# One layer of a hybrid backbone on one NeuronCore: k's heads moved to banks that q's copies leave free, and GpSimd's subtractions cut in four

## The reference

```python
shift_a, scale_a, gate_a, shift_f, scale_f, gate_f = modulation(silu(c) @ w_ada + b_ada)   # w_ada: 1024 x 6144
h = rmsnorm(x, g_pre_mix) * (1.0 + scale_a) + shift_a
z = h @ w_in                                    # u | q | k | v | o, 512 columns each, and 16 gate columns
y_pool = pool_mixer(u, w_pool, pool_scale)      # box means over 2, 4, 8, 16 positions
y_ml, C, n, m = mlstm_mixer(q, k, v, o, gate_pre, b_gate, C0, n0, m0)   # 4 heads, forward and backward
x = x + gate_a * rmsnorm(concat(y_pool, y_ml) @ w_out, g_post_mix)
h = rmsnorm(x, g_pre_ffn) * (1.0 + scale_f) + shift_f
x = x + gate_f * rmsnorm(moe(h), g_post_ffn)    # 64 experts, top 6 of 4 groups, and one shared expert
```

## Time and profile before

| what | value |
|---|---|
| median of three runs | 725.77 us (725.65 to 727.65) |
| the profiled execution | 726.23 us, of which the span of the engines' work is 724.1 us |
| PE busy | 685.0 us, 95% of the span |
| DVE busy | 384.5 us, 53% |
| ACT busy | 194.1 us, 27% |
| POOL busy | 89.1 us, 12% |
| HBM | 254.64 MB read, 357 GB/s over the span |
| granted clock of PE, mean | 0.994 |

### The profile page before, as it was taken

The page is one execution under the profiler, slowest core; times in us unless marked ns, Lnnn a source line. Parts: engine busy times, 40 slices in busy tenths (PEclk is TensorE's granted clock), DMA queues, the critical chain, the costliest instruction groups (busy, mean ns, idle before and its releaser), DMA issues.

```text
span 724.1 us, 11495 instructions
## 1 busy us (share of the span) xinstructions
PE 685.0 (95%) x4263; PEld 395.1 (55%) x4263; DVE 384.5 (53%) x979; ACT 194.1 (27%) x335; POOL 89.1 (12%) x53
## 2 busy tenths in 40 slices
PE   2799999989999999999999999999999999999993
PEld 2588888767865735545444545454445445444431
DVE  3458989694298354454444445454445436442115
ACT  3245344563371302112111111211111121130103
POOL 2453655313213000000000000000000000000000
PEclk9999999999999999999999999999999999999997
DMA  9999875815489479999999999999999999999994
GB/s 316 382 350 340 260 245 221 296 55 175 146 329 426 204 290 417 428 423 427 393 386 428 421 425 424 423 425 424 425 424 427 423 425 426 423 426 421 419 410 189
DMA packets 51013, 259.16 MB, mean 358 GB/s; under 512 B 6704, under 2 KB 9312, under 8 KB 32904
## 3 DMA queue, kind: packets, MB, share of 16 engines
q1 hardware_dynamic: 46816, 252.50, 86.6%
q0 software_dynamic: 1584, 4.90, 2.0%
q10 hardware_dynamic: 2552, 0.98, 0.5%
HBM read 254.64 MB, written 3.71 MB: 357 GB/s over the span
## 4 chain that ended last, share of the span: by engine, by line
PE 66%; DMA 14%; DVE 12%; SPq 3%; issue 2%; ACT 2%; POOL 0%; DVEq 0%; ACTq 0%
PE psum L2495 22%; PE psum L2503 10%; PE psum L2383 9%; PE psum L2467 8%; DMA w_gu<-in_w_expert_gu 7%; DVE psum L1329 4%; DMA w_gu<-in_w_in 3%; PE psum L2344 3%; DMA w_dn<-in_w_expert_down 2%; DMA w_gu<-in_w_ada 2%; PE psum L2395 2%; SPq L800 1%; PE psum L604 1%; PE psum L2454 1%; PE psum L2067 1%
## 5 line engine op out<-in xcount | busy, mean ns | idle before, releaser
L2495 PE MATMUL psum<-w_gu,hgT 128*32 128x512 f32 (+1 forms) x1280 | 191.4, 594 | 2.5 <-DMA w_gu<-in_w_expert_gu 2.5
L2495 PEld LDWEIGHTS psum<-w_gu,hgT 128*32 128x32 f32 (+1 forms) x1280 | 57.9, 119 | 127.7 <-issue 127.6
L1782 DVE TENSOR_TENSOR f_acc<-f_acc,psum 128x512 f32<-128x512 f32 x132 | 86.7, 684 | 43.3 <-PE psum L2467 43.3
L2503 PE MATMUL psum<-w_dn,actT 128*32 128x512 f32 (+1 forms) x640 | 98.7, 596 | 1.4 <-DMA w_dn<-in_w_expert_down 0.9
L1760 DVE SCALAR_TENSOR_TENSOR act<-sil,wsl,psum 128x256 f32<-128x256 f32 x27 | 18.4, 681 | 127.6 <-ACT sil L1127 118.3
L589 POOL TENSOR_TENSOR w_lo<-w_gu,w_hi 128x2048 fp32r<-128x2048 f32 x13 | 59.9, 4606 | 71.4 <-ACT w_hi L881 71.4
L2383 PE MATMUL psum<-onehot,h_lo 128*128 128x512 f32 (+1 forms) x168 | 66.6, 397 | 0.0
L2383 PE MATMUL psum<-onehot,h_hi 128*128 128x512 f32 (+1 forms) x168 | 65.4, 389 | 0.0
L2503 PEld LDWEIGHTS psum<-w_dn,actT 128*32 128x32 f32 (+1 forms) x640 | 27.0, 119 | 58.5 <-issue 57.7
L1766 DVE TENSOR_TENSOR y_lo<-psum,y_hi 128x1024 fp32r<-128x1024 f32 x26 | 31.8, 1224 | 50.8 <-ACT y_hi L1131 50.8
L1127 ACT ACTIVATE sil<-psum 128x256 f32<-128x256 f32 x27 | 10.4, 384 | 173.7 <-PE psum L2495 173.7
(11 more groups left out here) (335 smaller groups left out, 846.5 us busy)
## 6 DMA issues: line engine op xcount, KB each, us to landing
w_gu<-in_w_expert_gu SPq DMA_DIRECT2D x49, 2048.0 KB, 17.3
w_dn<-in_w_expert_down SPq DMA_DIRECT2D x61, 1024.0 KB, 15.1
w_gu<-in_w_expert_gu SPq DMA_DIRECT2D x27, 1024.0 KB, 15.9
w_gu<-in_w_ada SPq DMA_DIRECT2D x12, 2048.0 KB, 13.4
w_gu<-in_w_in SPq DMA_DIRECT2D x4, 2048.0 KB, 10.2
w_gu<-in_w_out SPq DMA_DIRECT2D x2, 2048.0 KB, 9.0
bc<-mod_rows POOLq DMA_DIRECT2D x6, 512.0 KB, 7.3
w_gu<-in_w_expert_gu SPq DMA_DIRECT2D x6, 512.0 KB, 20.4
```

The source lines that it names most:

```text
L1782: v.tensor_tensor(dst, dst, bank(5 + n), ALU.add).then_inc(f_added, 1)
L2495: ins = t.matmul(bank(target)[rows, :], column(c)[:, rows], w_gu[s][:, c, :], start=(c == 0), stop=(c == NC - 1), tile_position=(0, rows.s ...
L2503: ins = t.matmul(bank(target + n)[rows, :], actT[:, j, rows], w_dn[s][:, j, 512 * n:512 * (n + 1)], start=(j == 0), stop=(j == 1), tile_po ...
```

## The change

1. `z_bank`: k's heads go to banks 4, 3, 2, 5 (before 2, 3, 4, 5), and v's, o's and u's tiles to 4, 3, 2 (before 2, 3, 4). Only k's third head now shares a bank with a head of q.
2. `ada(4)` is moved from between q and k to between the halves of k. Its result goes to bank 1 (before bank 6), and it waits for the first copy of q (before for DVE's `abs_ready`). On DVE `ada_sums(5)` goes ahead of `ada_evac(4)`.
3. `low` subtracts in four pieces of 128 x 512 (before one of 128 x 2048). PE still waits for all four pieces of a half. The last half of w1 is divided as before.
4. ACT rounds k's second half (`high(3)`) after two of q's four copies (before after all four).
5. `g_nat` is one tile of 72 rows: rows 0 to 3, 32 to 35 and 64 to 67 hold the backward rows of the three quantities (six DVE copies), and the four rows after each of these the forward rows, which three transfers on ACT's queue bring (before nine DVE copies). A token tile is then transposed by one product (before three), and two DVE copies put its columns in order (before one).

```diff
@@ z_bank
-            return (1, 2, 0, 7)[i] if w == "q" else 2 + i
+            return {"q": (1, 2, 0, 7), "k": (4, 3, 2, 5)}.get(w, (4, 3, 2))[i]
@@ low
+        PIECES = 4
...
-            cs = slice(4 * half, 4 * half + 4)
             engine.wait_ge(w_hi_ready, k + 1)
-            engine.tensor_tensor(w_lo[s][:, cs, :], w_gu[s][:, cs, :], w_hi[half][:, :, :].bitcast(F32), ALU.subtract)\
-                .then_inc(w_lo_ready, 1)
+            for j in range(PIECES):
+                c = 4 * half + j
+                engine.tensor_tensor(w_lo[s][:, c, :], w_gu[s][:, c, :], w_hi[half][:, j, :].bitcast(F32), ALU.subtract)\
+                    .then_inc(w_lo_ready, 1)
@@ scalar
-            for n in range(4):
-                z_evac(n)
+            z_evac(0)
+            z_evac(1)
             high(3)
+            z_evac(2)
+            z_evac(3)
...
+            a.wait_ge(w_ready, 2)
+            for n, rows in enumerate((g_u, g_b, g_t)):
+                a.dma_start(g_nat[32 * n + H:32 * n + 2 * H, :], rows[0:H, :]).then_inc(nat_ready, 16)
@@ vector
-            ada_evac(4)
             ada_sums(5)
+            ada_evac(4)
...
-                v.tensor_copy(g_nat[0:32, n, :], rows[0:32, :]).then_inc(nat_ready, 1)
-                v.tensor_copy(g_nat[32:36, n, 0:T_CTX], rows[32:36, natural(1, 0)]).then_inc(nat_ready, 1)
-                v.tensor_copy(g_nat[32:36, n, T_CTX:T], rows[32:36, T - 1:T_CTX - 1:-1]).then_inc(nat_ready, 1)
+                here = slice(32 * n, 32 * n + H)
+                v.tensor_copy(g_nat[here, 0:T_CTX], rows[32:36, natural(1, 0)]).then_inc(nat_ready, 1)
+                v.tensor_copy(g_nat[here, T_CTX:T], rows[32:36, T - 1:T_CTX - 1:-1]).then_inc(nat_ready, 1)
@@ tensor, ada
-                if i == 4:
-                    t.wait_ge(abs_ready, 1)
-                if i > 4:
-                    t.wait_ge(z_act, 4)
+                if i >= 4:
+                    t.wait_ge(z_act, 1 if i == 4 else 4)
@@ tensor, z_chunk
-                    t.wait_ge(w_lo_ready, SPLIT.index((w, half)) + 1)
+                    t.wait_ge(w_lo_ready, PIECES * (SPLIT.index((w, half)) + 1))
...
                     if half == 0:
                         ins.then_inc(half_used, 1)
+                        if w == "k":
+                            ada(4)
@@ tensor, gates_T
-                for a_ in range(3):
...
+                t.matmul(bank(1, col, col + 24), g_nat[:, P * tile:P * tile + P],
+                         ident[0:72, 0:96].rearrange("p (a r) -> p a r", a=3)[:, :, 0:2 * H],
+                         start=True, stop=True).then_inc(gT_done, 1)
```

More of the change, by code:

```diff
@@ L328, in build_layer @@
         w_pool = at("w_pool", [P, len(WINDOWS), P], BC + 21248)
-        g_nat = at("g_nat", [36, 3, T], BC + 15104)
+        g_nat = at("g_nat", [72, T], BC + 17408)
         bc = at("bc", [P, 6, D], BC)
@@ L357, in ada_direct @@
         def ada_direct(i):
-            j = 3 if i == 4 else i % 4
-            return bank(6 + i % 2, P * j, P * j + P)
+            if i == 4:
+                return bank(1, 0, P)
+            return bank(6 + i % 2, P * (i % 4), P * (i % 4) + P)
         def ada_out(i):
@@ L953, in _ @@
             high(7)
-            a.wait_ge(gT_ready, 1)
+            a.wait_ge(gT_ready, 2)
             a.activation(emT[:, :, :], gT[:, 1, :, :], ACT.Exp, scale=-1.0).then_inc(em_ready, 1)
@@ L1236, in _ @@
             own.add(v.memset(gate_sum[:, :], 0.0))
+            own.add(v.memset(g_nat[:, :], 0.0))
             own.add(v.memset(v1[:, :, :, DH:DV], 1.0))
@@ L1315, in ada_sums @@
                         v.wait_ge(z_act, 4)
-                        v.wait_ge(mod_ready, 5)
+                        v.wait_ge(abs_ready, 1)
                     elif i == 9:
@@ L1356, in _ @@
             v.tensor_tensor(g_b[:, :], g_b[:, :], g_mx[:, :], ALU.add).then_inc(scans_ready, 1)
+            ada_sums(5)
             ada_evac(4)
-            ada_sums(5)
             v.wait_ge(scans_ready, 1)
@@ L1367, in _ @@
             v.wait_ge(gT_done, NT)
-            v.tensor_copy(gT[:, :, :, :].rearrange("p a i r -> p (a i r)"), bank(1, T, T + 72)).then_inc(gT_ready, 1)
+            rows_T = bank(1, T, T + 72).rearrange("p (i a r) -> p a i r", i=NT, a=3)
+            for d in range(2):
+                v.tensor_copy(gT[:, :, :, H * d:H * d + H], rows_T[:, :, :, H * (1 - d):H * (1 - d) + H]).then_inc(gT_ready, 1)
             ada_evac(5)
@@ L1958, in _ @@
             g.wait_ge(mxhi_ready, 3)
-            g.wait_ge(w_lo_ready, 8)
+            g.wait_ge(w_lo_ready, PIECES * 8)
             for n, (rows, dst, src) in enumerate(MAXIMA):
@@ L2021, in ada_total @@
                 if i >= 6:
-                    t.wait_ge(gT_ready, 1)
+                    t.wait_ge(gT_ready, 2)
                 for m in range(2):
@@ L2086, in q_low @@
             def q_low(heads, half):
-                t.wait_ge(w_lo_ready, half + 1)
+                t.wait_ge(w_lo_ready, PIECES * (half + 1))
                 for h in heads:
@@ L2169, in z_chunk @@
                         ins.then_inc(half_used, 1)
+                        if w == "k":
+                            ada(4)
             def gates_T(tile):
-                t.wait_ge(nat_ready, 9)
-                for a_ in range(3):
-                    col = T + 24 * a_ + 8 * tile
-                    ins = t.matmul(bank(1, col, col + 2 * H), g_nat[:, a_, P * tile:P * tile + P],
-                                   ident[0:36, 0:64].rearrange("p (d r) -> p d r", d=2)[:, :, 0:H],
-                                   start=True, stop=True)
-                ins.then_inc(gT_done, 1)
+                t.wait_ge(nat_ready, 6 + 16 * 3)
+                col = T + 24 * tile
+                t.matmul(bank(1, col, col + 24), g_nat[:, P * tile:P * tile + P],
+                         ident[0:72, 0:96].rearrange("p (a r) -> p a r", a=3)[:, :, 0:2 * H],
+                         start=True, stop=True).then_inc(gT_done, 1)
             def keys_T():
@@ L2291, in wo_step @@
                     ins.then_inc(wo_done, 1)
-            t.wait_ge(w_lo_ready, SPLIT.index(("w0", 0)) + 1)
+            t.wait_ge(w_lo_ready, PIECES * (SPLIT.index(("w0", 0)) + 1))
             t.wait_ge(tl_ready, len(PARTS) + 1)
@@ L2313, in _ @@
             mixed_T(2)
-            t.wait_ge(w_lo_ready, SPLIT.index(("w0", 1)) + 1)
+            t.wait_ge(w_lo_ready, PIECES * (SPLIT.index(("w0", 1)) + 1))
             for i in range(NT):
@@ L2318, in _ @@
                 wo_step(0, 1, i)
-            t.wait_ge(w_lo_ready, SPLIT.index(("w1", 0)) + 1)
+            t.wait_ge(w_lo_ready, PIECES * (SPLIT.index(("w1", 0)) + 1))
             wo_step(1, 0, 0)
             wo_step(1, 0, 1)
-            t.wait_ge(w_lo_ready, LAST_HALF + 1)
+            t.wait_ge(w_lo_ready, PIECES * LAST_HALF + 1)
             t.wait_ge(w_lo_last, 1)
```

2 lines of the change are left out of this document (removed).

## The result

| | before | after |
|---|---|---|
| median | 725.75 us (20 runs) | 728.59 us (727.37 to 731.78, 20 runs) |
| ratio, 95% interval | | 1.0038 [1.0027, 1.0049] |
| profiled execution, its span | 726.23, 724.1 us | 728.84, 726.9 us |
| PE busy | 685.0 us | 685.0 us |
| POOL busy | 89.1 us, 12% | 97.2 us, 13% |

The changed kernel is slower by 2.8 us: inside the predicted range, but by its median past the 0.3% that "no change" was to mean (the interval begins at 0.27%). All of it is there when PE comes to `ada_total(9)`: from that point to the end of the span before took 593.8 us and after 593.6.

A forecast was written before the change was run, and what follows sets the result against it. PE's and DVE's chains were taken to end together at `ada_total(9)`, 0.51 us apart. PE starting o 1.3 us later, less that wait, gave 0.8 us slower: about 726.6 us median, range 723.8 to 728.9.

The forecast's parts named there:

- The pieces' own time: On POOL, a piece of 512 columns takes 1.27 us, four take 5.1 us, 0.5 us more than one subtraction.
- The charge for DVE's two operations: Two small DVE operations let in between pieces hold POOL up 0.35 us each, 0.7 us in all.
- What the pieces bring: DVE's long waits shrink to the rest of one piece, 0 to 1.3 us; scans end some 5 us earlier.
- 1.7 of the 1.9 us of removed gaps: Ahead of k and v on PE: POOL's slower pieces eat 1.7 us, leaving v 0.2 us earlier.
- k's start: On PE, k starts when POOL is done, at 55.8 us instead of 57.92, 2.1 us earlier.
- a4's move and SP: a6's issue 9.5 us later, landing and constants 5.2 us later; o issued at 79.5 us, started 1.3 us later.
- Rival A: SP's hanging issue falls away, o comes in time, PE goes on 1.5 us earlier: 723.9 us, chance 0.18.
- rival B: Queue serves o and a7 side by side, o lands in 12.2 us: 3.8 us slower, 729.6 us, chance 0.17.
- edits at nothing: g_nat's memset, three transfers on ACT's queue (at most 0.43 us each), gT's second copy and high(3)'s order cost nothing.
- The transpositions: On PE between v and o, three steps of about 0.3 us instead of 0.76: 1.4 us off.
- DVE at `ada_total(9)`: a8 issued at 92.5 us, landing in 13.1 us, DVE done about 128.3 us; PE's 0.51 us wait goes.

The follow-up runs named there:

- E7: Kernel before with only GpSimd's subtraction of a half split into four pieces: 723.62 us, ratio 0.9970.
- E5: Changed kernel with GpSimd's subtraction of a half again in one instruction instead of four pieces: 731.13 us, ratio 1.0083.
- E2: Changed kernel with ACT's seven DMA issues behind the rounding of v's first half instead of ahead of it: 730.44 us, ratio 1.0060.
- E4: Changed kernel with five instead of three unread products keeping PE busy ahead of q: 728.42 us, ratio 1.0039.
- E10: Changed kernel with six unread products on PE filling the gap ahead of v's first product: 728.65 us, ratio 1.0033.
- E6: Changed kernel with a4's product back between q and k, still in bank 1 and waiting for q's first copy: 726.02 us, ratio 0.9998.
- E9: Kernel before with four pieces and a4's product moved between k's halves, into bank 1; k's banks old: 732.11 us, ratio 1.0079.
- E11: Changed kernel with a4 wholly as before (place, bank 6, wait, DVE order) and ACT's seven issues behind high(4): 722.20 us, ratio 0.9945.
- E1: Changed kernel with SP's seven constants issued behind a7 instead of behind a6: 730.57 us, ratio 1.0065.
- E12: Changed kernel with a4 wholly as before, the g_nat transfers on POOL's queue ahead of half 4, ACT's other four issues unmoved: 722.59 us, ratio 0.9962.
- E3: Changed kernel with SP's constants behind a7 and ACT's seven issues behind v's first rounding: 731.14 us, ratio 1.0073.
- E8: Changed kernel with ACT's seven issues behind high(4) and SP's seven constants behind a8: 732.57 us, ratio 1.0087.

## Why the prediction came out as it did

**The pieces' own time** was right: 1.26 us each, 5.04 us for four that nobody disturbs (1.27 and 5.1 predicted). The charge for DVE's two operations was 0.7 us, and eight pieces took 10.53 us instead of 10.08, so 0.45.

**What the pieces bring** was mis-sized twice. I let the scans end 5 us earlier, by taking each long wait down to the rest of one piece. They end 1.7 us earlier, since with pieces not two operations wait but six. And I let 1.7 of the 1.9 us of removed gaps be eaten by POOL; E7 shows k 2.2 us earlier with the pieces alone, by way of ACT. The pieces are worth 2.2 us against the kernel before (E7) and 2.5 to 3.3 us inside the change (E5).

**k's start**: predicted 1.7 us after q's end, measured 1.37, behind POOL's last piece as the text has it.

**a4's move and SP.** The order of events was right, the size was not. It is read best where no fall at q shifts the start, in E2, E4 and E10. a6 is issued at 65.2 to 65.6 us (predicted 66.2) and lands at 74.2 to 74.8 (74.1). The pool scales' issue comes free at 75.1 to 75.5 (74.8), but the issues behind it then take 5.5 to 5.9 us instead of 4.7. So o is issued at 80.9 to 81.4 us (79.5), lands at 90.5 to 90.6 (88.7), and PE starts it at 97.5 to 97.7 (95.9). The end of the last constant's issue was to move by 5.2 us and moved by 6.5 to 7.0. This term was too small: o starts some 1.7 us later than the sum has it. Rival A, o in time, and rival B, o in 12.2 us, fell: o took 8.9 us in after. (A's own sum has a slip: issued at 75.6 us, o lands 9.2 us later at 84.8, not at 86. Its result does not hang on that.) By the ratios a4's move costs 2.9 us inside the change (E6) and 7.9 on top of the pieces, with the old banks (E9).

The idle stretch of the load queue, 5 us near 65 us, does not measure the loss. The kernel before had one of 6 us near 91 us, and in neither was it the queue that a8 waited for: it was issued when DVE's sums of a6 ended (94.75 us, before) and when v ended (96.42 us, after). What counts is which load comes late, and who waits for it.

**ACT's issues** stood under "edits at nothing", as "three issues like the one of 0.43 us". This step failed. They took 1.25, 0.63 and 0.58 us, wait for ACT's last exponential, and the four issues behind them took 2.7 us (2.1 before). So from the scans' end to `high(4)` went 6.3 us instead of 2.3. I had counted on scans that end 5 us earlier and had not looked at what v's half had to spare: 0.06 us. The 4.0 us met a gain of 1.7; the half's four pieces took 0.4 us more than one, PE was through with k 0.3 us earlier after q's end, and so v waited 2.91 us. While o is later still, that gap only comes out of the one before o (0.93 us instead of the 2.8 predicted): in E2 it is closed, and o starts no earlier. With a4 back it counts: E6 has a gap of 2.06 us there with a fall at it, and E11, with the issues late, neither.

**The transpositions**: 0.30 us a step, as taken.

**DVE at `ada_total(9)`**: the wait of 0.51 us was to go, and is 0.52. a8 was to be issued at v's end, at 92.5 us. It was issued at 96.42, because v ended later, and took 14.4 us instead of 13.1. The missed gap before v set v's end, and so this term too. But 92.5 was out of reach in any case: a8 takes the buffer of a6, and DVE's sums of a6 ended at 94.97 us. In before and in E7 it is these sums that a8 waits for, and not v.

**The clock** had no term in the sum. Before shows no fall until 715.6 us; after shows one at q, and E4 shows that it did not move o. From o's start to `ada_total(9)` E4 took 35.35 us, where the prediction had 35.2. So the 2.97 us of after are the 0.8 of the sum, about 1.7 for o's later start and 0.5 for DVE's wait. That the time stayed within the range is owed to the range's width and not to these terms. A fall behind o does cost: E9 and E10 have 36.8 us there, 1.4 to 1.5 more than E4.

**What stays open.** Why the profile of after has no fall behind its own gap of 2.91 us before v, where E1, E4 and E6 fell behind 2.49, 3.02 and 2.06 us at the same place. How much of the 2.9 us between E6 and after is the late load and how much the clock, since no run held the clock with a4 in k. What the slower executions of E1, E6, E10 and E12 have that the faster ones lack: each run has one profile. And of the 3.8 us between E6 and E11, how much is ACT's issues and how much a4's bank, its wait and its order on DVE, since no run changed one of them alone with a4 before k.

## What to carry to other kernels

Before moving a product that frees a load buffer, follow the buffer: which issue waits for it, what stands behind that issue in an in-order queue, and which engine needs that first. Here o stood eight issues behind a6, and it was issued 6 us later. Where issues are only put into another order (E1, E3, E8), look for who waits next.

An edit may be put at nothing only if the chain it lies on has been measured. Three small issues on ACT met a chain with 0.06 us of slack.

When a kernel's PE chain is nearly closed, a new gap of 2 us can cost twice, once as a wait and once as slow products behind it. And a bundle of five edits may hold a good one: here a4's move and ACT's issues cost more than the pieces, the new banks and the one-tile gates gained (E11 722.2, E7 723.6, before 725.8, the bundle 728.6).
